# One core of Trainium2, hybrid pooling and stick-breaking attention layer: when VectorE and GpSimd close an attention row

## The reference, cut to what matters

```python
SEQ, D_MODEL, N_HEADS, HEAD_DIM, Q_BLOCK = 2048, 1024, 8, 64, 128
...
logits = einsum('bqhd,bkhd->bhqk', q_blk, kf) * inv_sqrt_d
mask = key_pos[None, :] < q_pos[:, None]
log_beta = log_sigmoid(logits)
log_1m_beta = where(mask, log_sigmoid(-logits), 0.0)
later = cumsum(log_1m_beta, axis=3, reverse=True) - log_1m_beta
wts = where(mask, exp(log_beta + later), 0.0)
out = einsum('bhqk,bkhd->bqhd', wts, vf)
```

## Time and profile before

| what | us |
|---|---|
| median of 3 runs | 1636.92 |
| lowest and highest | 1635.85, 1638.66 |
| the profiled execution | 1635.96 |
| its span, first to last instruction | 1634.2 |
| TensorE busy | 1586.9 (97%) |
| VectorE busy | 1134.6 (69%) |
| GpSimd busy | 906.3 (55%) |
| ScalarE busy | 755.8 (46%) |
| the attention stage | about 400 to 1265 |

### The profile page before, as it was taken

How to read it: one execution, slowest core, us unless ns; L and a number is a source line. 1 busy time by engine, 2 the same in 40 slices (tenths; PEclk the granted TensorE clock), 3 DMA queues, 4 the chain that set the end, 5 groups by cost and what they waited for, 6 DMA issues and landing times. The chain is left out here.

```text
span 1634.2 us, 24931 instructions
## 1 busy us (share of the span) xinstructions
PE 1586.9 (97%) x8030; PEld 1321.3 (81%) x8030; DVE 1134.6 (69%) x1554; ACT 755.8 (46%) x1448; POOL 906.3 (55%) x665
## 2 busy tenths in 40 slices
PE   7999999999999999999999999999999899999998
PEld 5877888788888887888887888888887688888886
DVE  7745425764989889998998988999887763333323
ACT  4422222224667665676665666666666431112111
POOL 3421112421789878888777897898874332314140
PEclk9999999999999999999999999999999999999999
DMA  7742336754434243452793333434314773534332
GB/s 257 233 134 106 129 116 194 250 156 143 140 94 114 82 139 86 114 139 76 242 334 104 107 97 102 119 91 140 100 43 142 220 228 111 165 108 149 116 103 77
DMA packets 150868, 228.82 MB, mean 140 GB/s; under 512 B 46929, under 2 KB 72017, under 8 KB 150754
## 3 DMA queue, kind: packets, MB, share of 16 engines
q1 hardware_dynamic: 150754, 227.42, 45.3%
HBM read 149.76 MB, written 77.60 MB: 139 GB/s over the span
## 5 line engine op out<-in xcount | busy, mean ns | idle before, releaser
L1593 DVE TENSOR_TENSOR_SCAN left<-keep,left 128x512 f32<-128x512 f32 x192 | 297.1, 1547 | 33.5 <-issue 22.4
L1420 PE MATMUL psum<-hT,ring 128*128 128x512 f32 x644 | 264.5, 411 | 5.2 <-DVE sum_d L1629 2.3
L1660 POOL TENSOR_TENSOR ring<-raw,ring 128x512 fp32r<-128x512 f32 x138 | 232.9, 1688 | 60.2 <-ACT ring L1500 45.7
L1424 PE MATMUL psum<-hT,ring 128*128 128x512 f32 x644 | 263.2, 409 | 0.0
L1422 PE MATMUL psum<-hT,ring 128*128 128x512 f32 x644 | 262.6, 408 | 0.0
L1506 ACT ACTIVATE keep<-psum 128x512 f32<-128x512 f32 (+3 forms) x320 | 170.5, 533 | 178.5 <-PE psum L1446 176.5
L1513 ACT ACTIVATE wt<-psum 128x512 fp32r<-128x512 f32 (+3 forms) x320 | 170.9, 534 | 110.8 <-PE psum L1454 107.9
L1466 PEld LDWEIGHTS psum<-wt,vm 128*128 128x128 f32 x1088 | 171.6, 189 | 32.8 <-issue 7.0
L1599 DVE TENSOR_TENSOR wt<-psum,wt 128x512 fp32r<-128x512 f32 (+3 forms) x320 | 189.7, 593 | 8.4 <-ACT wt L1513 5.9
L1466 PE MATMUL psum<-wt,vm 128*128 128x256 f32 x1088 | 182.5, 282 | 5.1 <-DVE row_sum L1608 4.3
L1454 PE MATMUL psum<-ident,left 128*128 128x128 f32 x1088 | 170.8, 272 | 1.4 <-DVE wt L1599 1.3
(11 more groups left out here) (181 smaller groups left out, 3231.3 us busy)
## 6 DMA issues: line engine op xcount, KB each, us to landing
raw<-in_w_strips SPq DMA_DIRECT2D x92, 256.0 KB, 4.1
qm<-qk_scratch SPq DMA_DIRECT2D x128, 128.0 KB, 4.1
gate<-gate_scratch SPq DMA_DIRECT2D x64, 256.0 KB, 4.0
hT<-form_scratch SPq DMA_DIRECT2D x28, 512.0 KB, 8.1
xt<-in_x SPq DMA_DIRECT2D x16, 512.0 KB, 5.2
xT<-in_x_T SPq DMA_DIRECT2D x16, 512.0 KB, 4.1
qk_scratch<-staging SPq DMA_DIRECT2D x32, 256.0 KB, 2.7
qk_scratch<-store_lo SPq DMA_DIRECT2D x32, 256.0 KB, 3.6
```

The lines of the kernel that those rows point to most:

```text
L1420: pe.matmul(o, hi, m_hi, start=k == 0, stop=False)
L1424: last = pe.matmul(o, lo, m_hi, start=False, stop=k == HK - 1)
L1593: dve.tensor_tensor_scan(left[:, n % LN, span][:, ::-1], k, k, carry, ALU.mult, ALU.bypass).then_inc(scanned, 1)
L1660: pool.tensor_tensor(out_, a, b, op).then_inc(s, 1)
```

## The change

A table gives each row's closing step. For rows with at least two items (i of 4 and more) it is one step later than before, n + 6; for the one-item rows it stays n + 5. VectorE's `add_halves` and GpSimd's `finish_row` go by the table. ScalarE's `other_half` stays at n + 5, and SP's `store_y` at n + 8.

```diff
     LAST = [n for n in range(ALL) if item(n)[5]]
+    ROW_END = {n: n + AV_LAG + (2 if item(n)[1] >= 4 else 1) for n in LAST}
...
                 if s < ALL:
                     scan(s)
-                if s - AV_LAG - 1 in LAST:
-                    add_halves(s - AV_LAG - 1)
+                for n in LAST:
+                    if s == ROW_END[n]:
+                        add_halves(n)
...
                 for u in at(V_HI, s):
                     if u >= VN:
                         value_lo(u)
-                if s - AV_LAG - 1 in LAST:
-                    finish_row(s - AV_LAG - 1)
+                for n in LAST:
+                    if s == ROW_END[n]:
+                        finish_row(n)
```

## The result

| | before | after |
|---|---|---|
| median, us (runs) | 1637.58 (6) | 1646.14 (6) |
| lowest and highest | 1635.84, 1638.66 | 1642.58, 1650.48 |
| the profiled execution, us | 1635.96 | 1642.58 |
| its span, granted clock | 1634.2, 0.994 | 1640.8, 0.995 |

The ratio after to before is **1.0057, 95% interval [1.0038, 1.0075]**: about 9 us slower. 1639.8 with the range 1635.3 to 1644.0 was forecast, so the median lies outside the range.

What follows compares the result with a forecast made beforehand. TensorE was taken to bound the kernel, so only its waits count. Terms -0.9 + 0.65 + 3.15 = +2.9 us, on the footing of the shown runs' median (1636.92), gave 1639.8 us, range 1635.3 to 1644.0.

Steps and rivals of the forecast that it cites:

- the eight rows i = 4: Rows before the one-item rows: two additions side by side around ScalarE's copy, leaving VectorE 0.98 us late.
- the ordinary rows: 88 of the 96 moved rows: TensorE's wait for the closed row is covered; gains minus 0.9, losses plus 0.65 us.
- the tails: Rows i = 4 to 0 ending each half of a pair; eight, numbered by time, near 510 to 1260 us: plus 3.15.
- Tails 3 and 4 at 0: Half ends near 724 and 829 us: cover of 1.28 us, and a VectorE gap of 0.52, absorb the lateness: 0.
- tail 2 at +0.98: Half end near 615 us: TensorE already waits 1.00 for row 1's addition, no slack: plus 0.98 us.
- The round trip (0.50): Between row 4's and row 3's additions VectorE stands still for ScalarE's copy of `half_sum`: 0.50 us.
- `y_out` of 0.45 in tails 5 and 7: Half ends near 938 and 1156 us: GpSimd's `y_out` of row 4 taken as short, 0.45 us; long gives 1.35 more each.
- the wait of over 1.5 us near 623: Sign expected in the changed profile: one TensorE wait for `row_sum` of more than 1.5 us there.
- GpSimd's order in tails 5 to 7: Half ends near 938 and 1156 us: row 4's `y_out` behind the ring's low part, plus 0.46 each; near 1046 not applied.
- Tail 1: Half end near 510 us: GpSimd's queue from row 1's addition to a value block's low part, slack 0.48: plus 0.65 us.
- Tail 6: Half end near 1046 us: VectorE's lateness of 0.98 less a swallowed `y_out` wait of 0.36 and 0.04: plus 0.6 us.
- The rival "cost double" (1643.8): `y_out` long near 938, 1046 and 1156 us (+4.0), or late scans colliding with GpSimd's; 1643.8 us, chance 0.25.

Runs made afterwards that it cites:

- the last kernel: Against the kernel before: rows i = 5 and more close one step later, in front of the scan; row 4 unmoved but also in front; ratios 0.9985, then 0.9972.
- the one at 1.0000: Against the change: VectorE's additions of all moved rows stand in front of the scan of step n + 6, not behind it; 1637.26 us, ratio 1.0000 to before.

## Why the prediction was wrong

- **What bounds the kernel: right.** TensorE's busy time in the stage hardly changed (838.5 and 839.0 us from the first `score` to the last) and idle time carried most of the difference; VectorE's 19.7 us less behind `half_sum` bought nothing.
- **The step that failed** is the sentence on the eight rows i = 4: "TensorE needs row 2's sum to weigh the first item of row 0, and row 1's to weigh the first item of the next half." The list left out row 4's own sum, which TensorE needs for row 2's item. The code rule was quoted (a row's first `weigh` waits for the row two before) and applied to the ordinary rows, "at least two steps after the old place, thus one after the new". Between row 4 and row 2 lies only row 3's one item: one step after the old place, none after the new. What it left out stood in the sum at nothing and measured plus 7.2 us in row 2's steps, against 3.15 forecast for the tails in all. The runs show it three ways: row 4 alone costs 1.0045, leaving it out 1.0002, and with its addition in front of the scan the seven waits are gone. The last brought back 3.6 of the 9.3 us; the rest needed GpSimd's order, or the other rows, changed as well.
- **Tails 3 and 4 at 0, tail 2 at +0.98**: follow from the same gap. The forecast looked only at row 1's addition, with 1.28 us of cover in tail 3, while the wait came at row 2's item, three steps earlier; and once TensorE is held there, the later wait that tail 2's sum rests on disappears (net +0.30).
- **The round trip (0.50) and `y_out` of 0.45 in tails 5 and 7: right.** The copy's wait reads 0.50 and the `y_out` 0.45. But the round trip was forecast to reach TensorE at row 1's addition, and it did not: the wait of over 1.5 us near 623 that was to show it is absent. The Trainium skill, SBUF — State Buffer, section "Who interferes with whom", says that an instruction of VectorE with two inputs in SBUF and a reading GpSimd instruction shut each other out for the whole instruction; the lengths agree here, since `y_out` takes 0.45 with VectorE waiting and 1.80 beside a scan.
- **GpSimd's order in tails 5 to 7**: the mechanism was right (TensorE's wait moved one step forward, to row 0's item). That tails 5 and 7 came to +0.55 and +0.83, near the forecast +0.46, is luck: row 0's step and the next one, which the forecast was about, sum to -0.56 and -0.52, and row 2's step, which it did not know, adds 1.11 and 1.35. Tail 1, at +1.06 for +0.65, is the same: all of it is at row 2's item. Tail 6 was mis-sized: +2.12 against +0.6. Its `y_out` of row 4 fell behind the ring's low part as in tail 5 (VectorE waits 1.77 there), while the forecast treated only VectorE's 0.98.
- **Ordinary rows.** The gains near 1008.7 and 1091 are there (-0.63 and -0.62 for -0.5 and -0.4), the losses near 962.6 and 1069.9 (+0.65) are not. Missing was +1.42 near 648, a wait at a transpose that grew from 0.67 to 1.45 us; the timeline of after shows VectorE's scan and GpSimd's products there:

```profile
645.93 1.28 POOL L1662 TENSOR_TENSOR staging<-staging,mix_t 128x512 f32<-128x512 f32 x1 [0.17 <-POOL y_out L1662]
646.30 1.99 DVE L1594 TENSOR_TENSOR_SCAN left<-keep,left 128x512 f32<-128x512 f32 x1
...
650.67 0.63 PE L1455 MATMUL psum<-ident,left 128*128 128x128 f32 x4 [1.45 <-DVE wt L1600]
```

  Before, the same scan took 1.39 and the same `staging` product 2.00: the two engines changed who waits for whom. It is in the kernel with GpSimd moved alone (1.45 at 649.80) and not in the one with VectorE moved alone, so GpSimd's move makes it. The forecast has no term for that move in ordinary rows ("GpSimd's addition moves with it"), an oversight of 1.4 us. The 1.70 near 686 is where the forecast saw the sum come earlier (near 682) and put 0. It came later: in after a scan of 2.32 and a SiLU product of 1.71 stand ahead of the sum, in before 1.71 and 1.33, and in the kernel with only row 4's addition in front 1.71 and 0.88. What makes them long in some kernels of this order and not in others stays open.
- **The rival "cost double" (1643.8)** had a total nearer to the truth by another mechanism: its long `y_out` did not occur. The profile's 6.6 us against the medians' 8.6 is not explained by any row here; the granted clock was 0.995 in the profiled execution, and 0.992 in three of the other five, the two slowest among them, so the clock may be a part of it.
- **The signs.** Those that came: VectorE's wait for `half_sum` below 12, nine more waits of ScalarE for `row_sum` (12 against 3), the waits at row 0's item in tails 5 and 7, the wait near 1008.7 gone. Those that did not: a wait for `row_sum` of 6 to 9 us (10.3), and the one near 623.

What stays open: whether a third PSUM bank for the rows' sums would remove the wait at row 2's item at its root. It wasn't tried: all eight banks are in use.

## What to carry to other kernels

Before a step is delayed, list every waiter of its semaphore at the **shortest** spacing that the loop ever has, not at the usual one, and look at what stands ahead of the step on its own engine in the step where the waiter comes: the rule "two rows earlier" left at least two steps in ordinary rows and one step behind row 4. If only few cases are short (8 of 96), exempt them; and put a delayed instruction in front of the long work of its new step rather than behind it, unless what it waits for comes late, since it then holds up the long work (row 4 in the last kernel). The change with row 4's step exempt and the additions in front went from 0.57% slower to 0.15 to 0.28% faster. And when a wait on a critical engine moves forward, take the later wait that it replaces off the sum.

## What the runs showed of the hardware

- Who wins a collision of VectorE and GpSimd shifts when a half-microsecond addition is moved: scans of the same 128x512 form take 1.28 to 2.25 us in the rows shown, GpSimd's product at the same place 1.28 and 2.00. Such a shift was worth 1.4 us at TensorE near 648.
- One kernel's runs spread over more than the effects studied: before went from 1631.53 to 1640.50 us in 23 runs on one chip. Some of it goes with the granted clock: the mean over the run was 0.998 in the fastest and 0.991 in one of the slowest (1640.20).
- Behind TensorE's waits of 2.19, 2.29 and 3.37 us for a DMA in the stage the granted clock was 0.51 to 0.60 in the stretches named above, and behind one of 1.26 it stayed at 1.00. The length of the wait does not decide it alone: behind one of 2.46 at the end of the stage in before (1265.58) it stayed at 1.00 too. The three waits cost more than their own length: two steps right behind the wait of 2.29 took 0.8 us more each before than in the last kernel, where the wait was 0.76 and the clock 1.00.
- Below 0.3% a single profile's span decides nothing; the kernel with row 4's addition in front had a span of 1637.8 and a ratio of 1.0035, and the one at 1.0000 a span of 1636.9.
